# A two-layer block kernel on one core: input rows turned block by block in one opening stage, and twelve instead of nine weight tiles beside the top-k choice of keys

## What is computed

```
# projections: h = x @ w_in, split by columns into the mixers' inputs and four gates of 1024 columns
# mixer d starts from columns 2168..2999 (six tiles of 128 columns and one of 64)
# mixer b: eight small heads score all earlier keys, the best 128 are kept
score = sum_h(relu(iq_h . ik / sqrt(32)) * iw_h) / sqrt(8)      # 512 x 512, causal
_, idx = top_k(score, 128)                                      # per query row
o_b = softmax(q . latent[idx] / sqrt(64) + bias[distance]) @ latent[idx]
# merge: for every mixer, with y its output
merged += sigmoid(x @ w_gate) * (y @ w_branch)                  # 8 tiles of 128 columns each
```

## Time and profile before

| | |
|---|---|
| median of 3 runs | 2412.63 us (2411.73 to 2413.72) |
| the profiled execution, its own time | 2409.47 us |
| its span in the trace | 2407.5 us |
| PE busy, weight loads busy | 2218.6 us (92%), 1667.5 us (69%) |
| DVE, ACT, POOL busy | 1349.8, 905.0, 122.2 us |
| mean granted clock of PE | 0.943 |

### The profile page before, as it was taken

The page is one execution under the profiler, slowest core; times in us unless marked ns, Lnnn a source line. Parts: engine busy times, 40 slices in busy tenths (PEclk is TensorE's granted clock), DMA queues, the critical chain, the costliest instruction groups (busy, mean ns, idle before and its releaser), DMA issues. The chain is left out here.

```text
span 2407.5 us, 30205 instructions
## 1 busy us (share of the span) xinstructions
PE 2218.6 (92%) x11296; PEld 1667.5 (69%) x11296; DVE 1349.8 (56%) x2395; ACT 905.0 (38%) x1527; POOL 122.2 (5%) x153
## 2 busy tenths in 40 slices
PE   6899998899997899996999889999989998999997
PEld 4687765566776566663777678888767767788886
DVE  2552446866445565653345586964444456778544
ACT  3521233133232666764333432332333434233223
POOL 0000001200000223220000000000000000000000
PEclk8785999999998899998999989999989999999999
DMA  5220431132324899985332213322423131241313
GB/s 163 85 80 1 115 106 44 56 98 66 106 77 175 294 369 355 370 317 196 118 104 41 66 62 106 101 88 88 145 92 115 56 77 52 74 133 62 110 49 114
DMA packets 218989, 296.45 MB, mean 123 GB/s; under 512 B 48861, under 2 KB 183085, under 8 KB 210617
## 3 DMA queue, kind: packets, MB, share of 16 engines
q1 hardware_dynamic: 213722, 286.09, 35.6%
q0 software_dynamic: 5120, 8.40, 1.1%
HBM read 283.12 MB, written 22.07 MB: 127 GB/s over the span
## 5 line engine op out<-in xcount | busy, mean ns | idle before, releaser
L1581 PE MATMUL acc<-x_hi,w_hi 128*128 128x512 f32 x1432 | 577.9, 404 | 19.7 <-DVE w_lo L1532 16.3
L1582 PE MATMUL acc<-x_lo,w_hi 128*128 128x512 f32 x1432 | 565.7, 395 | 0.0
L1583 PE MATMUL acc<-x_hi,w_lo 128*128 128x512 f32 x1432 | 564.8, 394 | 0.0
L1502 ACT CAST w_hi<-raw 128x1024 fp32r<-128x1024 f32 x179 | 186.9, 1045 | 620.0 <-PE acc L1583 585.3
L1532 DVE TENSOR_TENSOR w_lo<-raw,w_hi 128x1024 fp32r<-128x1024 f32 x174 | 212.8, 1224 | 292.3 <-ACT w_hi L1502 289.3
L1581 PEld LDWEIGHTS acc<-x_hi,w_hi 128*128 128x128 f32 x1432 | 273.4, 191 | 84.6 <-DVE w_lo L1532 17.4
L1583 PEld LDWEIGHTS acc<-x_hi,w_lo 128*128 128x128 f32 x1432 | 272.6, 190 | 59.9
L1582 PEld LDWEIGHTS acc<-x_lo,w_hi 128*128 128x128 f32 x1432 | 273.5, 191 | 58.1 <-issue 2.0
L1186 DVE TENSOR_TENSOR w_lo<-wgu,w_hi 128x1024 fp32r<-128x1024 f32 x128 | 150.7, 1219 | 66.4 <-ACT w_hi L1144 63.0
L1144 ACT CAST w_hi<-wgu 128x1024 fp32r<-128x1024 f32 x128 | 128.0, 1047 | 43.9 <-DMA wgu<-in_moe_w_up 36.9
L1117 PE MATMUL ps<-wd,y 128*64 128x512 f32 x256 | 116.7, 598 | 0.7 <-DVE y L1202 0.7
(11 more groups left out here) (561 smaller groups left out, 3411.2 us busy)
## 6 DMA issues: line engine op xcount, KB each, us to landing
raw<-in_w_in SPq DMA_DIRECT2D x60, 1024.0 KB, 5.6
raw<-in_w_gate SPq DMA_DIRECT2D x40, 1024.0 KB, 5.3
wgu<-in_moe_w_gate SPq DMA_DIRECT2D x32, 1024.0 KB
wgu<-in_moe_w_up SPq DMA_DIRECT2D x32, 1024.0 KB
wd<-in_moe_w_down SPq DMA_DIRECT2D x32, 1024.0 KB
raw_b<-in_w_branch SPq DMA_DIRECT2D x56, 256.0 KB, 2.7
room<-in_w_out SPq DMA_DIRECT2D x3, 2048.0 KB, 8.0
y_t<-in_w_out SPq DMA_DIRECT2D x3, 2048.0 KB, 10.3
```

What stands on the lines that cost most here:

```text
L1502: self.nc.scalar.copy(self.w_hi[n % 2], self.weights(n)).then_inc(self.rounded, 1)
L1581: pe.matmul(acc, hi, tile.hi[:, k, :], start=(k == 0), stop=False)
L1582: pe.matmul(acc, hi, tile.lo[:, k, :], start=False, stop=False)
L1583: mm = pe.matmul(acc, lo, tile.hi[:, k, :], start=False, stop=(k == KT - 1))
```

## The change

The opening stages `load`, `fill_with` and `rows_to_split` become one stage. SP issues the identity, then x in four row blocks, each with its own semaphore, then the first weight group, then (behind DVE's two fills) the seven tables, the rest of the constants, and the second and third weight group. PE transposes a row block when it is there, in halves of four column blocks; ACT and DVE follow by halves. The stage waits for the identity and the rows only; the tables and the other constants are waited for in `delta_lead`, by DVE after its part of the first tile and by PE after the second tile.

```diff
-def rows_to_split(c, rows, x_hi, x_lo):
+def rows_to_split(c, consts, x, rows, x_hi, x_lo, opening, tables, tables_in, fills):
+            @block.sync
+            def _(sp):
+                sp.dma_start(c.consts[:, 0:first], consts[:, 0:first]).then_inc(ident_in, 16)
+                for i in range(NT):
+                    sp.dma_start(rows[:, i, :], x[i * P:(i + 1) * P, :]).then_inc(rows_in[i], 16)
+                for dst, src, loaded in opening[:1]:
+                    sp.dma_start(dst, src).then_inc(loaded, 16)
+                sp.wait_ge(filled, len(fills))
+                for dst, src in tables:
+                    sp.dma_start(dst, src).then_inc(tables_in, 16)
+                sp.dma_start(c.consts[:, first:], consts[:, first:]).then_inc(tables_in, 16)
+                for dst, src, loaded in opening[1:]:
+                    sp.dma_start(dst, src).then_inc(loaded, 16)
             @block.tensor
             def _(pe):
-                for k in range(KT):
-                    if k >= 5:
-                        pe.wait_ge(split, k - 4)
-                    for i in range(n):
-                        mm = pe.transpose(ps[:, k % 5, i * P:(i + 1) * P], rows[:, i, k * P:(k + 1) * P], c.const("ident"))
-                    mm.then_inc(turned, 1)
+                pe.wait_ge(ident_in, 16)
+                for i in range(NT):
+                    pe.wait_ge(rows_in[i], 16)
+                    for half in range(2):
+                        if 2 * i + half >= 5:
+                            pe.wait_ge(split, 2 * i + half - 4)
+                        for k in range(4):
+                            mm = pe.transpose(turned_rows(i, half)[:, k, :], rows[:, i, (4 * half + k) * P:(4 * half + k + 1) * P],
+                                              c.const("ident"))
+                        mm.then_inc(turned, 1)
...
@@ delta_lead, tensor
                     if n == tiles[1]:
+                        pe.wait_ge(*tables_in)
@@ delta_lead, vector
-                nc.vector.tensor_tensor(lb_logits[:, 1], lb_logits[:, 1], lb_logits[:, 0], ALU.subtract).then_inc(diff, 1)
                 for n in tiles:
                     stream.dve(dve, n)
+                    if n == tiles[0]:
+                        dve.wait_ge(*tables_in)
+                        nc.vector.tensor_tensor(lb_logits[:, 1], lb_logits[:, 1], lb_logits[:, 0], ALU.subtract).then_inc(diff, 1)
```

```diff
@@ selection_stage
-        rounds, per = 3 * KEEP // 8, 6
+        work = sum((8 + 2 * KEEP // 8) * (i + 1) for i in range(1, NT))
...
+                done, left = 0, list(fill)
+                def share(i, ops):
+                    nonlocal done
+                    if left and done * len(fill) >= (len(fill) - len(left)) * work:
+                        stream.product(dve, left.pop(0) - 1)
+                    done += ops * (i + 1)
                 for i in range(1, NT):
                     for h in range(8):
+                        share(i, 1)
...
                     for _r in range(KEEP // 8):
-                        if taken % per == 0:
-                            stream.product(dve, fill[taken // per] - 1)
+                        share(i, 2)
...
-                for n in fill[(rounds + per - 1) // per:]:
+                for n in left:
                     stream.product(dve, n - 1)
@@ first_block
-                    selection_stage(c, stream, merge_d + merge_a[0:1], pj[:, 2:4], pj[:, 4], ik, kv_gain[:], lat, lat_t[:],
+                    selection_stage(c, stream, merge_d + merge_a[0:4], pj[:, 2:4], pj[:, 4], ik, kv_gain[:], lat, lat_t[:],
-                attention_stage(c, stream, [], merge_a[1:], units, HD ** -0.5)
+                attention_stage(c, stream, [], merge_a[4:], units, HD ** -0.5)
```

More of the change, by code:

```diff
@@ L198, in const @@
         return self.consts[0:rows, o:o + w]
[L202 to L213, removed]
+def rows_to_split(c, consts, x, rows, x_hi, x_lo, opening, tables, tables_in, fills):
     nc = c.nc
+    first = LAY["ident"][0] + LAY["ident"][1]
@@ L217, in transpose_many @@
     with ExitStack() as ctx:
[L218 to L225, removed]
-        with c.stage() as block:
+        ps = c.ps(ctx, "tp", [P, 5, 512])
+        ident_in, turned, rounded, split, filled = (c.sem(x) for x in ("ident_in", "turned", "rounded", "split", "filled"))
@@ new lines, in rows_to_split, with turned_rows @@
+        rows_in = [c.sem("rows_in") for _ in range(NT)]
+        def turned_rows(i, half):
+            return ps[:, (2 * i + half) % 5, :].rearrange("p (k t) -> p k t", t=P)
+        with c.stage() as block:
+            @block.sync
[11 more added lines that the diff above has]
+                    sp.dma_start(dst, src).then_inc(loaded, 16)
@@ L239, in _ @@
+            @block.scalar
+            def _(act):
+                for i in range(NT):
+                    for half in range(2):
+                        act.wait_ge(turned, 2 * i + half + 1)
+                        nc.scalar.copy(x_hi[:, 4 * half:4 * half + 4, i * P:(i + 1) * P], turned_rows(i, half)).then_inc(rounded, 1)
             @block.vector
             def _(dve):
-                for n in range(0, len(items), 2):
-                    dve.wait_ge(turned, n + 1)
-                    nc.vector.tensor_copy(*result(n)).then_inc(out_v, 1)
@@ new lines, in _ @@
+                for t, value in fills:
+                    nc.vector.memset(t, value).then_inc(filled, 1)
+                for i in range(NT):
+                    for half in range(2):
+                        k = slice(4 * half, 4 * half + 4)
+                        dve.wait_ge(rounded, 2 * i + half + 1)
+                        nc.vector.tensor_tensor(x_lo[:, k, i * P:(i + 1) * P], turned_rows(i, half),
+                                                x_hi[:, k, i * P:(i + 1) * P].bitcast(F32), ALU.subtract).then_inc(split, 1)
@@ L1357, in _ @@
                                                     x_hi[:, k, i * P:(i + 1) * P].bitcast(F32), ALU.subtract).then_inc(x_split, 1)
[L1360 to L1366, removed]
 def column(v):
@@ L2358, in copied_rows, with delta_lead @@
                    ap=[[1024, 4], [0, P], [1, wide]])
-def delta_lead(c, stream, tiles, tables, onehot, rows_dram, strips, strips_in, lb_logits, lbs, lbs_dram, memory):
+def delta_lead(c, stream, tiles, tables, onehot, tables_in, rows_dram, strips, strips_in, lb_logits, lbs, lbs_dram, memory):
     nc = c.nc
@@ L2901, in first_block @@
                     stream.into(tiles, [pj[:, j] for j in range(6)] + [low])
-                    load(c, [(c.consts[:], a["consts"]), (x_rows[:], x_from)])
-                    stream.open()
-                    fill_with(c, [(a2, 0.0), (tables[32:33, :], 1.0)])
-                    c.load_beside([(tables[0:32, 0:8], a["rpb_table"]), (tables[0:32, 8:12], a["rel_bias_2"]), (onehot[:], a["strips"])]
-                                  + [(lb_logits[:, l, 2 * w:2 * w + 2], column(a["hg_lb_logits_2"][l, w])) for l in range(2) for w in range(2)])
-                    rows_to_split(c, x_rows, x_hi, x_lo)
+                    bias_tables = ([(tables[0:32, 0:8], a["rpb_table"]), (tables[0:32, 8:12], a["rel_bias_2"]), (onehot[:], a["strips"])]
+                                   + [(lb_logits[:, l, 2 * w:2 * w + 2], column(a["hg_lb_logits_2"][l, w])) for l in range(2) for w in range(2)])
+                    rows_to_split(c, a["consts"], a["x"][0], x_rows, x_hi, x_lo, stream.opening(), bias_tables, tables_in,
+                                  [(a2, 0.0), (tables[32:33, :], 1.0)])
                     c.load_beside([(col[n][:], column(a[n][0])) for n in names]
@@ L2912, in first_block @@
                     c.to_fetch += mem_in
-                    delta_lead(c, stream, tiles, tables, onehot, dram["bias_rows"],
+                    delta_lead(c, stream, tiles, tables, onehot, (tables_in, 16 * len(bias_tables) + 16), dram["bias_rows"],
                                [dram[n] for n in ("strips_a", "strips_b", "strips_w")], strips_in, lb_logits, lbs[:], dram["lbs"], memory)
                     stream.close()
+                    c.fresh.append(tables_in)
                 r, k, v = pj[:, 0:2], pj[:, 2:4], pj[:, 4:6]
```

12 lines of the change are left out of this document (1 added, 11 removed).

## The result

The changed kernel takes 2391.01 us (median of 4 runs, 2383.89 to 2391.96), the kernel before 2412.18 us (4 runs beside it, 2408.95 to 2413.72). The ratio is 0.9913, with a 95% interval from 0.9896 to 0.993: 21 us faster, where I had forecast 2387 (2381 to 2396). The profiled execution is the fastest of the four, at 2383.89 us with a span of 2382.1; its span is 25.4 us shorter than that of before, 2407.5.

What follows compares the result with a forecast made beforehand. PE, busy 92% of the span, was taken as the bound, with DVE's rounds bounding the choice of keys. Terms -13.6 + 5.7 - 17.7 = -25.6 us from 2409.47 gave 2383.9, plus 3.2 to the median: 2387 us, range 2381 to 2396.

Steps and rivals of the forecast that it cites:

- The opening: From the start to the first projection matmul: 14.8 us instead of 28.4, 13.6 us gained.
- the barrier at 12.4: End of the opening stage, with SP through its issues soon after the first weight group lands at 11.1; ends 11.5 and 17.6.
- No gain is booked: Opening: PE's clock falls in the idle stretch as before, since the new one is as long; nothing counted for it.
- the queue holds the opening stage: Rival, opening: SP stands until the second weight group has landed; gain 8.4 us, time 2392, chance 0.12.
- The choice of keys: Stage with three more tiles of 7.31 us on PE: no product late, DVE and PE end together, 5.7 us lost.
- PE keeps its clock: Choice of keys: with both engines ending together, PE does not fall to the low clock.
- The ports: Rival, choice of keys: three further POOL splits delay DVE's head sums, DVE ends 4.6 us behind PE; 2391.7 us, chance 0.06.
- The attention stage: Stage with three tiles fewer: 6.4 us freed by each, less one clock fall of 1.5 us; 17.7 us gained.
- 0.9 us of cover for each tile: Attention stage: each removed tile turns a covered step of 2.0 us into a bare one of 2.9 us.
- The extra fall: Attention stage: longer gaps between tiles bring one more fall of PE to 1.2 GHz, a loss of 1.5 us.
- The rival of the covered units: Attention stage: removed tiles hid more DVE work than booked; gain 13.2 instead of 17.7 us, time 2391.5, chance 0.15.
- Slower: Rival, choice of keys: DVE and PE wait for each other, clock stays at 1.2 GHz; 2431 us at six tiles, chance 0.02.

Runs made afterwards that it cites:

- Experiment 4: The changed kernel with the second and third weight group issued first in the next stage instead of in the opening one; 2388.55 us, timed again 2384.72 us.
- Experiment 3: The changed kernel, twelve tiles beside the choice of keys, with a product call before every sixth round as before instead of by shares; 2404.1 us, ratio 0.9969.
- the repetition: The changed kernel timed again, unchanged; 2389.79 us, ratio 0.9901.

## Why the prediction was right, step by step

- **The opening, -13.6 forecast, -10.25 measured.** Right: x is turned as it lands, the tail behind it is short, tables and constants are in time, nothing in the next stage waits for them. Off by 1.1: the last split at 12.64 instead of 11.5. The forecast let x and the identity land at 8.2, as if no load issued behind them moved beside them (its own working gives 8.0: 2.0 + 6.0). The last block landed at 9.6: by then 272 GB/s x 9.6 us = 2.6 MB had arrived, not the 2.16 MB counted. PE turned without a pause for 5.53 us from 5.26 and was just through with the third block then; the last eight transpositions and the tail took 3.0 us for 3.3. The step that failed in the main is the barrier at 12.4. I took "SP is through soon after" the first group has landed; SP was through at 15.39, and the cast came at 15.81. Experiment 4 takes that issue out of the stage and gets 2.5 us of it back. The rest of the 3.4 (first cast at 13.29, 0.9 later than 12.4) is the first group's landing, which the forecast had at 11.1. Of the 10.25 us, 9.84 reach the choice of keys. "No gain is booked" for the clock hides a small loss: behind the first matmul PE ran at half speed for 4.4 us (before 2.8), and the first tile took 7.8 us from its start to the next one's instead of 7.0. The rival "the queue holds the opening stage" (gain 8.4) named the mechanism; its size lay beyond the measured one by 1.9 us, my own value by 3.4. It was the nearer of the two.
- **The choice of keys, +5.7 forecast, +7.5 measured.** Right: 7.31 us a tile, no product late, DVE and PE ending 1.6 us apart with PE the bound. Experiment 3 shows that the calls by shares do this; with the old calls 15.1 us are lost. The missing 1.8 us are small sums. The branch product of the third tile stands at 402.50, 35.17 us into the stage where before had it at 34.65: +0.5, the clock's fall less what the first tile saved. Nine tiles and the third block's scores then took 472.83 - 402.50 = 70.3 us for 70.1. I ended the stage 1.31 us behind the start of the last branch product, as if a tile followed, but it runs for 1.88: +0.6. And the barrier opened 0.85 us behind PE's end instead of 0.33, behind SP's last issue, which the working didn't have: +0.5. "PE keeps its clock" holds from the third tile on.
- **The ports** came out as the forecast had it in total, and the rival (DVE ends behind PE, 2 us lost for each added split) is refuted. The 21 head sums of the stage after, by line (ns min/median/max, first and last start), which answer to the earlier trace rows:

```profile
L2506 DVE SCALAR_TENSOR_TENSOR masks<-rel,iw,masks x21: 484/619/2652, 373.4 to 443.2; 128x256 f32<-128x256 f32 x7, 128x384 f32<-128x384 f32 x7, 128x512 f32<-128x512 f32 x7
```

  The longest took 2.65 us for 0.62. The seven over 384 keys come to 6.6 us in all and the seven over 512 keys to 6.4 (before: 6.3 and 7.3). Four of them ran long here (2.65, 0.85, 1.69 and 0.98 us) where before two did (2.63 and 2.78), and the time lost is no more. The added splits fell beside rounds, and those ran no longer for it: the search for the eight largest over 512 keys took 0.70 us with POOL at work and without.
- **The attention stage, -17.7 forecast, -22.6 measured** (-19.4 in the repetition). Two terms failed here. The first is 0.9 us of cover for each tile, 2.7 in all: PE's wait for `probs_n` rose by 0.2 us, from 6.0 to 6.2. A step behind another takes as long as before (2.74 us in the two rows above, 2.87 in the earlier trace rows), so what I had misread is the step behind a tile: I took its 2.0 us, from one stretch of the earlier trace rows, for DVE's work covered by the tile. Why it is shorter stays open. The second is the fall of the clock. Three tiles are 3 x 7.31 = 21.9, and the old stage's one fall, priced at 1.5 us, is gone in the profiled run: 23.4, of which 22.6 were measured. The extra fall that I had booked did not come in this run, nor one behind every gap, which would have cost 3 us more. Here the profiled run was lucky: in the repetition the stage has two falls of 3.4 us each, a loss of 3.4, and is 3.2 us longer. The rival of the covered units (13.2) is refuted by both runs.
- **The sum.** -25.6 forecast and -25.0 measured within the profiled runs is better than its terms, and that is luck: the opening and the choice of keys gave 5.6 us less (as they reach the stage's start), the attention stage 4.9 more, and the two errors cancel. Between the medians it is 21.2. The median lies 4 us above the forecast because the +3.2 between profiled run and median, taken from before, was 7.1 here. Of the 7.1 the repetition shows 3.2, the falls in the attention stage that the profiled run had not; where the rest lies no profile shows.
- **Slower** did not happen, and DVE's 7 waits for PE (9.1 us) cost nothing: in this stage PE waited for no product.

## What to carry to other kernels

A stage closed by a barrier on all engines lasts as long as its slowest queue, and an issue behind many others is not free (4.75 us for two loads here): keep in the stage only the loads that it needs, and put the prefetch first into the next one (2.5 us here). When work is interleaved by hand, look at where the calls fall when the number of tiles changes. Spacing them by the work that lies between them was worth 15 us here against the old spacing, the whole gain from moving the tiles; whether an even spacing by count would have done as well was not run. Before thinning out the large matmuls of a stage, look at the clock in it: with four to two of them left the sum of both stages no longer fell, and with none (one run) the clock stayed at half and the sum was 15 us longer.

## What the runs showed of the hardware

- In the one profile with no large matmuls left in the stage, TensorE stayed at 1.2 GHz from 505 us to the stage's end at 560, and the profile has it busy for 95% of that time (50.54 of 53.00 us read). With two tiles left it fell to a mean of 0.60 in 505 to 520 us and was back at 1.00 from 520 on; with four it fell in four of seven profiles, for 3.4 to 6.8 us in all, and in three not at all.
- The same stage of the same kernel took 69.0 us with no fall of the clock and 72.2 with two. Between single runs this difference is larger than the 2.5 us that experiment 4 is worth.
- SP's issue of two 1 MB groups took 4.75, 1.89 or 6.76 us. The same two loads behind the same ones took 4.2 to 5.0 in seven profiles; issued later, 1.4 and 1.9; issued earlier, 6.76.
